# Norm roots as columns at the latent seam: statistics, root and reciprocal with tokens on partitions, turned back by TensorE, and two latent blocks interleaved

## The reference

```python
x1 = x + gate * (p @ w_ple_proj)                      # end of the first block
h = rms_norm(x1, norm_final)                          # input of the second block
u = rmsnorm(h, g_pre)
c_q, c_kv, k_pe, z_b = u @ w_in_2 (256, 128, 32, 512 columns)   # and the rwkv branch and gates
q = rmsnorm(c_q, g_q) @ w_uq ;  kv = rmsnorm(c_kv, g_kv) @ w_ukv
q_pe, k_pe = rope(q_pe, cos(pos * f), sin(pos * f)), rope(k_pe, ...)
o = softmax(causal((q_nope k_nope^T + q_pe k_pe^T) * scale)) v     # 8 heads
out = h + rmsnorm(merged @ w_o, g_post)
```

## Time and profile before

| | |
|---|---|
| median of 3 runs | 2646.39 us (2644.91 to 2657.43) |
| the profiled execution | 2648.93 us |
| its span, first to last instruction | 2647.1 us |
| mean granted TensorE clock | 0.995 |
| busy: TensorE, DVE, ACT, POOL | 2576.0, 1379.4, 793.9, 1206.0 us |
| the stretch of the change | about 1497 to 1580 us of the span |

### The profile page before, as it was taken

The page is one execution under the profiler, slowest core; times in us unless marked ns, Lnnn a source line. Parts: engine busy times, 40 slices in busy tenths (PEclk is TensorE's granted clock), DMA queues, the critical chain, the costliest instruction groups (busy, mean ns, idle before and its releaser), DMA issues.

```text
span 2647.1 us, 52353 instructions
## 1 busy us (share of the span) xinstructions
PE 2576.0 (97%) x21632; PEld 2033.5 (77%) x21632; DVE 1379.4 (52%) x1484; ACT 793.9 (30%) x1170; POOL 1206.0 (46%) x1415
## 2 busy tenths in 40 slices
PE   8999999999999999999999989999999999999999
PEld 6777778888777888878888767777777777777787
DVE  7654421115675565642246675553656455453874
ACT  4433310002433333321023435553131312212331
POOL 7543334446776656566576541123223222232550
PEclk9999999999999999999999999999999999999999
DMA  3111101113121221262122200001111111113441
GB/s 137 41 33 33 33 27 53 48 48 143 64 86 73 79 93 65 103 238 103 48 71 80 93 27 25 16 24 66 34 39 46 39 48 40 38 62 115 166 150 56
DMA packets 46994, 184.23 MB, mean 70 GB/s; under 512 B 6256, under 2 KB 6768, under 8 KB 42608
## 3 DMA queue, kind: packets, MB, share of 16 engines
q1 hardware_dynamic: 30240, 106.01, 11.7%
q10 hardware_dynamic: 16592, 75.77, 7.5%
HBM read 145.06 MB, written 36.70 MB: 69 GB/s over the span
## 4 chain that ended last, share of the span: by engine, by line
PE 76%; POOL 7%; issue 7%; DVE 6%; ACT 2%; DMA 2%; ACTq 0%; POOLq 0%; DVEq 0%; SPq 0%
PE dps L332 33%; PE dps L350 14%; PE aps L2423 6%; POOL ff_w L1251 6%; PE dps L1189 3%; PE aps L3215 2%; PE dps L1892 2%; PE aps L1984 2%; PE dps L693 2%; PE dps L2005 1%; PE dps L684 1%; PE aps L671 1%; PE dps L1997 1%; PE aps L1954 1%; PE aps L1189 1%
## 5 line engine op out<-in xcount | busy, mean ns | idle before, releaser
L3398 POOL TENSOR_TENSOR w_hi<-w_raw,one 128x256 fp32r<-128x256 f32 (+1 forms) x542 | 380.4, 733 | 1199.2 <-PE dps L332 514.9
L3403 POOL TENSOR_TENSOR w_lo<-w_raw,w_hi 128x256 fp32r<-128x256 f32 (+1 forms) x542 | 513.9, 979 | 0.5
L332 PE MATMUL dps<-h_hi,w_hi 128*128 128x512 f32 x832 | 265.6, 394 | 15.2 <-POOL w_lo L3403 11.0
L1189 PE MATMUL dps<-op,ff_w 128*128 128x512 f32 x1122 | 273.0, 393 | 1.8 <-DVE op L1014 1.8
L332 PE MATMUL dps<-h_lo,w_hi 128*128 128x512 f32 x832 | 262.5, 390 | 0.0
L332 PE MATMUL dps<-h_hi,w_lo 128*128 128x512 f32 x832 | 262.4, 390 | 0.0
L1189 PEld LDWEIGHTS dps<-op,ff_w 128*128 128x128 f32 x1122 | 212.7, 190 | 48.2 <-DVE op L1014 2.7
L1251 POOL TENSOR_TENSOR ff_w<-w_raw,ff_w 128x256 fp32r<-128x256 f32 x132 | 142.8, 1109 | 139.4 <-ACT ff_w L1238 139.4
L332 PEld LDWEIGHTS dps<-h_hi,w_hi 128*128 128x128 f32 x832 | 156.0, 189 | 53.3 <-POOL w_lo L3403 11.0
L332 PE MATMUL dps<-hid,w_hi 128*128 128x512 f32 x676 | 182.0, 391 | 4.8 <-DVE x_res L1430 3.1
L332 PEld LDWEIGHTS dps<-h_hi,w_lo 128*128 128x128 f32 x832 | 156.7, 188 | 33.0
(11 more groups left out here) (559 smaller groups left out, 4862.9 us busy)
## 6 DMA issues: line engine op xcount, KB each, us to landing
w_raw<-w_stream SPq DMA_DIRECT2D x192, 512.0 KB, 3.5
hid_t<-ff_up ACTq DMA_DIRECT2D x11, 1024.0 KB, 3.9
hid_raw<-hid_t ACTq DMA_DIRECT2D x22, 512.0 KB, 5.4
gates<-gate_out ACTq DMA_DIRECT2D x16, 512.0 KB, 2.6
gate_ring<-gates ACTq DMA_DIRECT2D x14, 512.0 KB, 4.6
x_res<-x_t ACTq DMA_DIRECT2D x2, 2048.0 KB, 8.8
x_res<-x_t ACTq DMA_DIRECT2D x4, 1024.0 KB, 7.3
x_t<-x_res ACTq DMA_DIRECT2D x4, 1024.0 KB, 4.0
```

What stands on the lines that cost most here:

```text
L332: mm = k.nc.tensor.matmul(k.dps[0:rows, pair, h * HALF:(h + 1) * HALF], w[:, slot, sub + t, 0:rows], x(t)[:, h * HALF:(h + 1) * HALF], sta ...
L1189: mm = k.nc.tensor.matmul(out, w[:, q, :], x, start=q == 0 and n == 0 and j not in (3, 5), stop=q == QUARTER - 1 and n == 2, skip_group_ch ...
L3398: g.tensor_tensor(k.w_hi[:, s, at], k.w_raw[:, s, at], ones, ALU.mult).then_inc(k.sem("w_hi_done"), 1)
L3403: return g.tensor_tensor(k.w_lo[:, s, at], k.w_raw[:, s, at], k.w_hi[:, s, at].bitcast(F32), ALU.subtract)
```

## The change

Sums are taken as columns: for each 128 tokens, the 128x128 tile of squares is the weight side and one column of "mean" the moving side, so that tokens lie on partitions and the statistics of 1024 tokens are 128x8 (`column`, `latent_stat`, `next_stat`). Root and reciprocal are made on 128x8. `turn_root` turns the result back: eight TensorE transposes whose weight side is the column broadcast over 128 columns, into 128x1024 of PSUM, from where ACT copies it (inv, inv_kv, the lower half of inv_q) or DVE multiplies it with trig (the upper half). std_x1 stays in SBUF as the 128x8 column; its DRAM tensor, spill and reload go. The DVE steps angle(3, 8) come ahead of the wait for inv. `latent_pe` takes three tiles of block 0, two of block 1, the other five of block 0, three of block 1, then the statistics and the rest of block 1; block 3 is taken in two parts around the second turn. The key product and the value product of DVE are separate, with the third reciprocal between them. Left out of the diff below are the signatures that lose std_t.

```diff
-    k.std_x1 = k.at("std_x1", C + 8 * kb, [S])
+    k.col_std, k.col_inv, k.std_x1 = (k.at(name, K + 4 * N_CONST + 32 + 1024 + 96 + 32 * n, [KT])
+                                      for n, name in enumerate(("col_std", "col_inv", "std_x1")))
...
+def column(k, pe, out, n, name, sums, start=True, stop=True):
+
+    a = CONST[name][0]
+    return k.nc.tensor.matmul(out[:, n:n + 1], sums[:, n * P:(n + 1) * P], k.const[:, a:a + 1], start=start, stop=stop, skip_group_check=True)
+
+
+def turned_column(k, n):
+
+    return k.col_inv[:, n:n + 1].to_broadcast([P, P])
+
+
 def next_stat(k, pe):
 
     pe.wait_ge(k.sem("sumsq_done"), KT * 4 + 2)
     pe.wait_ge(k.sem("sumsq_next_done"), KT + 1)
-    for h in range(2):
-        t = slice(h * HALF, (h + 1) * HALF)
-        k.nc.tensor.matmul(k.aps[:, h, :], const(k, "mean"), k.sumsq_next[:, t], start=True, stop=False)
-        k.nc.tensor.matmul(k.aps[:, h, :], const(k, "mean_eps"), k.sumsq[:, t], start=False, stop=True)
-    for h in range(2):
-        mm = k.nc.tensor.matmul(k.aps[:, 2 + h, :], const(k, "mean"), k.sumsq[:, h * HALF:(h + 1) * HALF], start=True, stop=True)
+    for n in range(KT):
+        column(k, pe, k.aps[:, 0, 0:KT], n, "mean", k.sumsq_next, stop=False)
+        column(k, pe, k.aps[:, 0, 0:KT], n, "mean_eps", k.sumsq, start=False)
+        mm = column(k, pe, k.aps[:, 0, KT:2 * KT], n, "mean", k.sumsq)
     mm.then_inc(k.sem("stat_done"), 1)
 
 
-def next_inv_act(k, act, std_t):
-    both = lambda n: k.aps[:, n:n + 2, :].rearrange("p a b -> p (a b)")
+def latent_stat(k, pe, bank, tiles):
+
+    for n in range(KT):
+        for at in tiles:
+            mm = column(k, pe, k.aps[:, bank, 0:KT], n, "mean", k.latent_sq[:, at, :], at == tiles[0], at == tiles[-1])
+    mm.then_inc(k.sem("latent_stat_done"), 1)
+
+
+def turn_root(k, pe, count, out):
+
+    pe.wait_ge(k.sem("col_inv_done"), count)
+    for n in range(KT):
+        mm = k.nc.tensor.transpose(out[:, n * P:(n + 1) * P], turned_column(k, n), const(k, "ident"))
+    mm.then_inc(k.sem("latent_stat_done"), 1)
+
+
+def root_dve(k):
+
+    k.nc.vector.reciprocal(k.col_inv[:, :], k.col_std[:, :]).then_inc(k.sem("col_inv_done"), 1)
+
+
+def far_sums(k):
+
+    return k.aps[:, 2:4, :].rearrange("p a b -> p (a b)")
+
+
+def next_inv_act(k, act):
     act.wait_ge(k.sem("stat_done"), 4)
-    k.nc.scalar.activation(k.std[:, :], both(0), ACT.Sqrt, bias=EPS * EPS).then_inc(k.sem("std_done"), 1)
-    k.nc.scalar.activation(k.std_x1[:, :], both(2), ACT.Sqrt, bias=EPS).then_inc(k.sem("std_x1_done"), 1)
-    act.wait_ge(k.sem("std_x1_done"), 1)
-    act.dma_start(std_t, k.std_x1[:, :]).then_inc(k.sem("std_spilled"), 16)
-
+    k.nc.scalar.activation(k.col_std[:, :], k.aps[:, 0, 0:KT], ACT.Sqrt, bias=EPS * EPS).then_inc(k.sem("std_done"), 1)
+    k.nc.scalar.activation(k.std_x1[:, :], k.aps[:, 0, KT:2 * KT], ACT.Sqrt, bias=EPS).then_inc(k.sem("std_x1_done"), 1)
+    act.wait_ge(k.sem("latent_stat_done"), 1)
+    k.nc.scalar.activation(k.inv[:, :], far_sums(k), ACT.Copy).then_inc(k.sem("inv_done"), 1)
 
 
 LATENT_USE = TILE["mla"] // 2
@@ -1732,36 +1765,44 @@
 def latent_pe(k, pe):
     b = BLK["mla"]
     mul = k.nc.tensor.matmul
-    later = lambda x: lambda t: x[:, t + 3, :]
-    dense(k, pe, b, 0, 0, rows(k.h_hi), rows(k.h_lo), KT, 0, LATENT_USE, "blk_done", ready=("h_lo_done", 4 * KT))
-    dense(k, pe, b + 1, 1, 0, rows(k.h_hi), rows(k.h_lo), 3, 1, LATENT_USE, None, last=False)
+
+    def part(blk, slot, lo, hi, pair, use, ready=None):
+        dense(k, pe, blk, slot, lo, lambda t: k.h_hi[:, t + lo, :], lambda t: k.h_lo[:, t + lo, :], hi - lo, pair, use,
+              "blk_done" if hi == KT else None, ready=ready, first=lo == 0, last=hi == KT)
+
+    part(b, 0, 0, 3, 0, LATENT_USE, ("h_lo_done", 4 * KT))
+    part(b + 1, 1, 0, 2, 1, LATENT_USE)
+    part(b, 0, 3, KT, 0, LATENT_USE, ("h_lo_done", 4 * KT + 3))
+    part(b + 1, 1, 2, 5, 1, LATENT_USE)
     next_stat(k, pe)
-    dense(k, pe, b + 1, 1, 3, later(k.h_hi), later(k.h_lo), KT - 3, 1, LATENT_USE, "blk_done", first=False)
-    dense(k, pe, b + 2, 0, 0, rows(k.h_hi), rows(k.h_lo), KT, 0, LATENT_USE + 1, "blk_done")
+    part(b + 1, 1, 5, KT, 1, LATENT_USE)
     pe.wait_ge(k.sem("std_done"), 4)
+    turn_root(k, pe, 1, far_sums(k))
+    part(b + 2, 0, 0, KT, 0, LATENT_USE + 1)
+    pe.wait_ge(k.sem("inv_done"), 4)
     pe.wait_ge(k.sem("std_x1_done"), 1)
     pe.wait_ge(k.sem("latent_sq_done"), 1)
-    for h in range(2):
-        mm = mul(k.aps[:, 2 + h, :], const(k, "mean"), k.latent_sq[:, 2, h * HALF:(h + 1) * HALF], start=True, stop=True)
-    mm.then_inc(k.sem("latent_stat_done"), 1)
+    latent_stat(k, pe, 2, (2,))
+    part(b + 3, 1, 0, 4, 1, LATENT_USE + 1)
+    pe.wait_ge(k.sem("latent_std_done"), 1)
+    turn_root(k, pe, 2, far_sums(k))
     pe.wait_ge(k.sem("pe_rot_done"), 1)
     for h in range(2):
         mm = mul(k.aps[:, h, :], const(k, "rope_sum", HD, P), k.pe_raw[HD:P, h * HALF:(h + 1) * HALF], start=True, stop=True)
     mm.then_inc(k.sem("pe_sum_done"), 1)
-    dense(k, pe, b + 3, 1, 0, rows(k.h_hi), rows(k.h_lo), KT, 1, LATENT_USE + 1, "blk_done")
+    part(b + 3, 1, 4, KT, 1, LATENT_USE + 1)
     pe.wait_ge(k.sem("w_split"), mla_block(0) + 1)
     pe.wait_ge(k.sem("pair0_out"), MLA_USE0 + 1)
     dense_half(k, pe, 0, 0, 0, 3 * KT, "mla_gate_near")
     pe.wait_ge(k.sem("latent_lo_done"), 1)
-    pe.wait_ge(k.sem("latent_std_done"), 1)
+    pe.wait_ge(k.sem("inv_kv_done"), 1)
     mla_keys_pe(k, pe, 0, 0)
     pe.wait_ge(k.sem("latent_sq_done"), 3)
     pe.wait_ge(k.sem("pe_key_done"), 1)
-    for h in range(2):
-        for n in range(2):
-            mm = mul(k.aps[:, h, :], const(k, "mean"), k.latent_sq[:, n, h * HALF:(h + 1) * HALF], start=n == 0, stop=n == 1)
-    mm.then_inc(k.sem("latent_stat_done"), 1)
+    latent_stat(k, pe, 0, (0, 1))
     dense_half(k, pe, 0, 1, 0, GATE_ENDS // 2)
+    pe.wait_ge(k.sem("latent_lo_done"), 3)
+    turn_root(k, pe, 3, k.dps[:, 1, :])
 
 
 def latent_dve(k, dve):
...
@@ -1785,10 +1826,12 @@
             dve.wait_ge(k.sem("angle_done"), n + 1)
 
     angle(0, 3)
-    inv_dve(k, dve, 3)
+    dve.wait_ge(k.sem("std_done"), 4)
+    root_dve(k)
+    angle(3, 8)
+    dve.wait_ge(k.sem("inv_done"), 4)
     dve.wait_ge(k.sem("pair0_out"), LATENT_USE + 2)
     v.tensor_tensor(k.pe_raw[HD:P, :], k.pe_raw[HD:P, :], k.inv[HD:P, :], ALU.mult).then_inc(k.sem("pe_scaled_done"), 1)
-    angle(3, 8)
 
     def take(n, pair, use):
         dve.wait_ge(k.sem("blk_done"), BLK["mla"] + n + 2)
@@ -1807,31 +1850,31 @@
     dve.wait_ge(k.sem("pe_scaled_done"), 1)
     v.tensor_tensor(k.pe_raw[HD:P, :], k.pe_raw[HD:P, :], k.trig[HD:P, :], ALU.mult).then_inc(k.sem("pe_rot_done"), 1)
     take(1, 0, LATENT_USE + 1)
+    dve.wait_ge(k.sem("latent_std_done"), 1)
+    root_dve(k)
     dve.wait_ge(k.sem("pe_sum_done"), 1)
     low(1, 0, "g_kv", 2)
     low(2, 0, "g_q", 0)
-    dve.wait_ge(k.sem("latent_std_done"), 1)
-    v.reciprocal(k.inv_kv[:, :], k.latent_std[:, 0, :]).then_inc(k.sem("latent_inv_done"), 1)
     take(2, 1, LATENT_USE + 1)
     low(3, 1, "g_q", 1)
-    dve.wait_ge(k.sem("std_spilled"), 16)
+    dve.wait_ge(k.sem("inv_kv_done"), 1)
+    dve.wait_ge(k.sem("mla_proj_done"), 1)
+    mla_key_dve(k)
+    dve.wait_ge(k.sem("latent_std_done"), 2)
+    root_dve(k)
+    mla_value_dve(k)
+    dve.wait_ge(k.sem("latent_stat_done"), 5)
+    v.tensor_tensor(k.inv_q[HD:P, :], k.dps[HD:P, 1, :], k.trig[HD:P, :], ALU.mult).then_inc(k.sem("latent_inv_done"), 1)
     dve.wait_ge(k.sem("latent_inv_done"), 1)
-    dve.wait_ge(k.sem("mla_proj_done"), 1)
-    mla_values_dve(k, dve)
-    dve.wait_ge(k.sem("latent_std_done"), 2)
-    v.reciprocal(k.inv_q[:, 0:HALF], k.latent_std[:, 1, 0:HALF]).then_inc(k.sem("latent_inv_done"), 1)
-    v.reciprocal(k.inv_q[:, HALF:], k.latent_std[:, 1, HALF:]).then_inc(k.sem("latent_inv_done"), 1)
-    dve.wait_ge(k.sem("latent_inv_done"), 3)
-    v.tensor_tensor(k.inv_q[HD:P, :], k.inv_q[HD:P, :], k.trig[HD:P, :], ALU.mult).then_inc(k.sem("latent_inv_done"), 1)
-    dve.wait_ge(k.sem("latent_inv_done"), 4)
-
-
-def latent_act(k, act, std_t):
+    dve.wait_ge(k.sem("inv_kv_done"), 2)
+
+
+def latent_act(k, act):
     a = k.nc.scalar
     act.wait_ge(k.sem("x1_spilled"), 64)
     act.wait_ge(k.sem("blk_done"), BLK["mla"] + 1)
     a.activation(k.pe_raw[HD:P, :], k.dps[HD:P, 0, :], ACT.Copy).then_inc(k.sem("pair0_out"), 1)
-    next_inv_act(k, act, std_t)
+    next_inv_act(k, act)
     act.wait_ge(k.sem("angle_done"), 8)
     a.activation(k.trig[:, :], k.angle[:, :], ACT.Sin).then_inc(k.sem("sin_done"), 1)
 
@@ -1840,18 +1883,21 @@
         a.activation(k.latent_sq[:, n, :], k.latent[:, n, :], ACT.Square).then_inc(k.sem("latent_sq_done"), 1)
         a.activation(hi[:, at, :], k.latent[:, n, :], ACT.Copy, scale=vec(k, gain, at)).then_inc(k.sem("latent_hi_done"), 1)
 
-    def root(n, bank, width):
-        act.wait_ge(k.sem("latent_stat_done"), n + 1)
```

(47 more changed lines are left out.)

## The result

The change makes the kernel slower by a quarter of a per cent: ratio 1.0028, 95% interval 1.0016 to 1.0041, medians 2654.43 us after and 2646.26 before (20 runs each). The forecast was 2648.1 with a range to 2651.4, so the side was right, the size not, and the time lies outside the range; it is within the half per cent to which the prediction gave 0.96. The ratio is 7.4 us of 2646. The profiled execution after took 2661.32 us, span 2659.5.

The account below looks back on a forecast made before the run. TensorE, busy 97% of the span, was taken as the bound. Terms 1.8 + 2.6 + 0.7 + 2.7 - 1.1 - 4.7 - 0.3 = +1.7 us gave a median of 2648.1 us, range 2641.8 to 2651.4.

Parts of the forecast that it names:

- the half per cent: Whole kernel: a change under 13.2 us, about what a measurement can tell from no change; no case reaches it.
- order of blocks and clock of the first gap: Before block 1's first matmul: TensorE waits for POOL's weight split, +1.8 us, and its clock falls, +2.6 us.
- angle first: DVE's angle(3, 8) ahead of the wait for the root removes TensorE's wait for latent_sq, -1.1 us.
- columns of next_stat and the first latent norm, two turns: First two statistics as one-column products, and two transposes of their roots on TensorE's queue at 0.9 us each.
- last statistic, third turn: The queries' statistic as 16 column products, and the transposes of its root, 0.9 us, on TensorE's queue.
- end of the seam: Between queries' product and mla_q: the wait behind the second reciprocal and inv_q's product goes, -4.7 us; bounds -4.7 and -3.3.
- chain behind mla_q: From mla_q to the first exponential, unchanged: a clock that stays up there gives back almost nothing, -0.3 us.
- second fall, at the exponential: Rival, chance 0.18: waiting 2 to 3 us for the first exponential drops TensorE's clock; +1.5 us and more, 2649.6.
- The statistics as columns: All three statistics: 96 column records at 0.115 us, 11.0 us, replace 24 records of 10.3 us; +0.7 us.
- The order of blocks: At block 1's early start: its weights, split by POOL, are late; start at 1503.8, cost +1.8 us, bounds 0 and 1.8.
- The clock: At the 5.7 us wait before block 1: TensorE works 5.1 us at half speed; +2.6 us, bounds 0 and 3.0.
- Turning the roots back: Three turns of eight 128x128 transposes on TensorE's queue, 0.9 us each, +2.7 us; roots hidden behind other work.

Follow-up runs that it names:

- order: The changed kernel with the blocks put back in the order of the kernel before; ratio to before 1.0001 (0.9986 to 1.0016).
- angle_only: The kernel before with only angle(3, 8) moved ahead of the reciprocal; ratio 1.0001 (0.9988 to 1.0014).
- wide_order: The changed kernel with 128 moving columns per statistics product and the old order of blocks; ratio to before 0.9989 (0.9978 to 1.0000).
- wide: The changed kernel with 128 moving columns instead of one in each statistics product; ratio to before 1.0000 (0.9992 to 1.0009), median 2645.24 us.
- last_thin: angle_only with only the queries' root turned, its 16 products having one moving column each; ratio 0.9995 (0.9983 to 1.0008), median 2646.89 us.
- last_wide: angle_only with only the queries' root turned, its 16 products having 128 moving columns each; ratio 0.9980 (0.9968 to 0.9992), median 2640.63 us.
- wide_order_again: The kernel of wide_order run once more, beside last_wide on the same chip; ratio 0.9992 (0.9976 to 1.0008).
- probe_thin: The kernel before plus 48 unread f32 products of one moving column behind block 1; one timed run 2663.2 us, beside 2646.27.
- probe_full: The kernel before plus 48 unread f32 products of 128 moving columns behind block 1; one timed run 2653.46 us, beside 2646.27.

## Why the prediction was wrong

The table gives each term a price by itself:

| step of the prediction | predicted | measured | from |
|---|---|---|---|
| order of blocks and clock of the first gap | +1.8 +2.6 | +4.54 | keys, after - order |
| angle first | -1.1 | -1.41 | keys, angle_only - before |
| columns of next_stat and the first latent norm, two turns | +0.5 +1.8 | +2.04 | keys, wide_order - angle_only |
| last statistic, third turn | +0.2 +0.9 | +0.93 | keys to queries, wide_order 7.20 for angle_only 6.27 |
| end of the seam | -4.7 | -4.83 | queries to scores, 4.39 for 9.22 |
| chain behind mla_q | -0.3 | -0.47 | scores to mla_p, 5.52 after for 5.99 before |
| clock falls in next_stat's columns | none | +3.24 | rope sum, order - wide_order |
| clock falls in the last columns | none | +3.23 | keys to scores, 14.84 after for 11.61 in wide |
| second fall, at the exponential | a rival, +1.5 | +1.64 | mla_p to rw_r, 237.92 for 236.28 |

These sum to 8.9 us, as measured (331.62 - 322.69). The prices come from different pairs of kernels, one profiled execution each.

- **The statistics as columns** is the step that failed. Its cadence was right: 0.115 us predicted, 0.112 measured, and one column and 128 take the same, as they would if the weight load set it. The 107 ns that the Trainium skill's rule (TensorE: Matmul & The Clock Gate, LDWEIGHTS) gives for a load of 128 columns is near these 112 ns. But the step priced 96 records at full clock, because the text looked for a fall only where TensorE waits. The records of one column let the clock fall without a wait, in the 48 of next_stat and in the 32 of the last norm, not in the 16 between. That is 6.5 us, where the measured sum lies 7.2 us above the predicted one (the second fall adds 1.6, and the other terms came out 0.9 lower). Last_thin against last_wide shows it in a kernel without the change's order of blocks and its other two turns.
- **The order of blocks** stood as written: POOL's split unmoved, block 1's start within 0.1 us of the forecast, 5.46 us of idle for 5.7, and a cost of 1.5 us for 1.8. **The clock** there cost more: it was low for 6.1 us of work, 3.1 us for 2.6; in wide, after the same wait, for 3.3 us, 1.65. So the price of one fall is uncertain by a factor of two: my bounds of 0 and 3.0 said so (3.1 is just beyond them), my single value did not. The fall in the last columns shows the same spread, 3.23 us here, 3.24 in last_thin and 1.67 in order.
- **Turning the roots back, angle first, the end of the seam, the chain behind mla_q** all came within about 0.3 us. No idle time stood at the latent statistics, mla_q (1584.00) started 0.04 us after the queries' last record ended (1583.34 + 0.62), and the six gate matmuls covered it.
- **The second fall** was put as an alternative, 0.18. It came, with the predicted price, on top of the rest. Why it comes is open: behind the same 1.98 us of idle time the clock fell in after, order, wide_order, last_wide and last_thin (237.8 to 237.9 us from mla_p to rw_r) and not in wide and wide_order_again (236.5, 236.4), of which the last is the same kernel as one that fell.

That the side was right is in part luck: in wide, where the falls that the sum had left out are gone (and the priced one took 1.65 us for 3.1), the ratio is 1.0000.

What no run tells apart is why 16 one-column records pass and 32 don't, and the 3.45 us that the profiled execution of after had lost ahead of the seam; I count those to the spread of executions. That last_wide beats wide_order is shown by the traces (2.0 us up to the first turn of mla_p) and not by the times, whose intervals overlap.

## What to carry to other kernels

Before you make a matmul thinner, see what sets its cadence: where each f32 product had its own 128-wide weight load, one moving column cost as much as 128, and the long groups of one-column products dropped TensorE's clock for what stood behind them. Price such a group by the granted clock in a window around it, not only by its instructions and its waits. And of a change with several parts, take the one part that removes a wait on the bound engine (here the last root, -4.8 us) and leave those that were hidden already (the first two, +2.0 us with their columns for nothing), and look up when the weights of a block are ready before starting it early.

## What the runs showed of the hardware

- TensorE at 20.00 busy of 20.00 us, its weight loads at 19.34, had a mean granted clock of 0.61 (probe_thin), the level of 1.2 GHz for most of it. With 128 moving columns in the same products it was 1.00 (probe_full). The Trainium skill (TensorE: Matmul & The Clock Gate, HAM oscillation — how this bites in real kernels) speaks of idle gaps as what brings a fall; this trace shows one with no gap, so a full queue is no proof that the clock stays up.
- In a stream of f32 products with a plain weight load of 128 columns each, a record takes 0.11 us at 2.4 GHz with one moving column or 128 (probe_thin, probe_full), and with one column 0.213 us at 1.2 GHz (the changed kernel's next_stat).
- A root on 128x8 took 0.18 us on ACT and a reciprocal 0.20 us on DVE, for 1.03 and 6.55 us on 128x1024. These are real savings of those engines, of which only the last root's lay on the path.
